# Two hybrid layers with paired heads, GpSimd scales and an earlier output projection, and a tail in halves

## The reference, cut to what matters

```python
p = rmsnorm(x, norm_g) @ w_in                       # 1024 -> 3488
(cq, ckv, kr, g_a, c_h, c_b, c_c, g_b, sg_u, sg_v, g_c, mq, mk, mv, g_d) = split(p)
q  = rmsnorm(rmsnorm(cq, .) @ mla_w_uq per head);   kv = rmsnorm(ckv, .) @ mla_w_ukv
o_a = causal_attention(rope(q), [rmsnorm(k_nope), rope(rmsnorm(kr))], v_a)   # 4 heads of 96
o_b = c_b * short_conv(c_c * c_h, conv_w)           # width 3, causal
o_c = sg_u * (tril(sg_w) @ layernorm(sg_v) + sg_b)  # chunks of 128 rows
o_d = causal_attention(rope(rmsnorm(mq)), rope(rmsnorm(mk)), mv)             # 4 heads of 64
x  = x + concat(o_a*silu(g_a), o_b*silu(g_b), o_c*silu(g_c), o_d*silu(g_d)) @ w_out
```

## Time and profile before

| | |
|---|---|
| median of 3 runs | 1792.18 us |
| profiled execution | 1790.85 us |
| its span, first to last instruction | 1788.9 us |
| TensorE busy | 1665.5 us, 93% |
| VectorE, ScalarE, GpSimd busy | 76%, 61%, 3% |
| mean granted TensorE clock | 0.966 |

### The profile page before, as it was taken

The page is one execution under the profiler, slowest core; times in us unless marked ns, Lnnn a source line. Parts: engine busy times, 40 slices in busy tenths (PEclk is TensorE's granted clock), DMA queues, the critical chain, the costliest instruction groups (busy, mean ns, idle before and its releaser), DMA issues.

```text
span 1788.9 us, 22550 instructions
## 1 busy us (share of the span) xinstructions
PE 1665.5 (93%) x7707; PEld 1374.0 (77%) x7707; DVE 1356.2 (76%) x1672; ACT 1086.1 (61%) x1308; POOL 47.8 (3%) x106
## 2 busy tenths in 40 slices
PE   6886987899899999799999999999999999999995
PEld 4665865688788888678888788888788887788884
DVE  4655675556654565789899799898898998898997
ACT  3343434356443446267777687777777777777773
POOL 2001000000100010100000000000000000000000
PEclk9897999799999999799999999999999999999998
DMA  9423542253454564359999899999899999899992
GB/s 331 140 94 94 172 137 75 77 188 104 156 177 155 187 217 135 125 201 370 381 352 371 302 357 372 355 370 347 312 371 376 358 360 350 310 371 368 363 359 105
DMA packets 153643, 462.71 MB, mean 259 GB/s; under 512 B 7807, under 2 KB 12173, under 8 KB 153405
## 3 DMA queue, kind: packets, MB, share of 16 engines
q1 hardware_dynamic: 151120, 454.32, 70.9%
q0 software_dynamic: 1696, 5.08, 1.1%
q10 hardware_dynamic: 716, 1.85, 0.3%
HBM read 460.18 MB, written 1.05 MB: 258 GB/s over the span
## 4 chain that ended last, share of the span: by engine, by line
PE 83%; DVE 7%; issue 4%; DVEq 3%; ACT 2%; POOL 0%; POOLq 0%; ACTq 0%
PE ps L2148 17%; PE ps L2150 17%; PE ps L2149 17%; PE ps L1686 8%; PE ps L1688 8%; PE ps L1687 8%; PE ps L2175 1%; PE ps L2082 1%; DVE wlo_sb L971 1%; PE ps L1711 1%; PE ps L2096 0%; PE ps L2097 0%; DVE wlo_sb L979 0%; ACT whi_sb L664 0%; PE ps L2067 0%
## 5 line engine op out<-in xcount | busy, mean ns | idle before, releaser
L979 DVE TENSOR_TENSOR wlo_sb<-raw_sb,whi_sb 128x1024 fp32r<-128x1024 f32 x672 | 788.3, 1220 | 111.2 <-ACT whi_sb L672 104.2
L672 ACT ACTIVATE whi_sb<-raw_sb 128x1024 fp32r<-128x1024 f32 x672 | 674.8, 1053 | 247.0 <-PE ps L2150 246.9
L2148 PE MATMUL ps<-whi_sb,xlo_sb 128*128 128x512 f32 x896 | 353.3, 394 | 9.8 <-issue 7.3
L2149 PE MATMUL ps<-wlo_sb,xhi_sb 128*128 128x512 f32 x896 | 350.3, 391 | 0.0
L2150 PE MATMUL ps<-whi_sb,xhi_sb 128*128 128x512 f32 x896 | 350.2, 391 | 0.0
L971 DVE TENSOR_TENSOR wlo_sb<-raw_sb,whi_sb 128x1024 fp32r<-128x1024 f32 (+2 forms) x198 | 225.5, 1180 | 160.7 <-ACT whi_sb L664 159.0
L664 ACT ACTIVATE whi_sb<-raw_sb 128x1024 fp32r<-128x1024 f32 (+2 forms) x198 | 192.2, 1021 | 238.9 <-PE ps L1688 212.8
L1686 PE MATMUL ps<-whi_sb,xlo_sb 128*128 128x512 f32 (+2 forms) x608 | 244.2, 402 | 21.3 <-DVE xlo_sb L1018 6.4
L1687 PE MATMUL ps<-wlo_sb,xhi_sb 128*128 128x512 f32 (+2 forms) x608 | 238.3, 392 | 0.0
L1688 PE MATMUL ps<-whi_sb,xhi_sb 128*128 128x512 f32 (+2 forms) x608 | 238.2, 392 | 0.0
L2148 PEld LDWEIGHTS ps<-whi_sb,xlo_sb 128*128 128x128 f32 x896 | 169.0, 189 | 46.7 <-issue 9.8
(11 more groups left out here) (353 smaller groups left out, 1414.8 us busy)
## 6 DMA issues: line engine op xcount, KB each, us to landing
raw_sb<-moe_wg SPq DMA_DIRECT2D x115, 1024.0 KB, 6.8
raw_sb<-moe_wu SPq DMA_DIRECT2D x112, 1024.0 KB, 7.0
raw_sb<-moe_wd SPq DMA_DIRECT2D x112, 1024.0 KB, 7.1
raw_sb<-w_in SPq DMA_DIRECT2D x40, 1024.0 KB, 5.1
raw_sb<-w_out SPq DMA_DIRECT2D x16, 1024.0 KB, 5.0
raw_sb<-ffn_wg SPq DMA_DIRECT2D x10, 1024.0 KB, 5.2
raw_sb<-ffn_wu SPq DMA_DIRECT2D x10, 1024.0 KB, 5.1
raw_sb<-ffn_wd SPq DMA_DIRECT2D x10, 1024.0 KB, 5.1
```

The costliest lines, as they stand in the source:

```text
L672: nc.scalar.activation(whi[i % SPLIT][:, c:c + KC // 2, :], raw[i % RAW][:, c:c + KC // 2, :], ACT.Copy).then_inc(hi_ready, 1)
L979: op = V.tensor_tensor(wlo[i % SPLIT][:, c:c + KC // 2, :], raw[i % RAW][:, c:c + KC // 2, :], whi[i % SPLIT][:, c:c + KC // 2, :], ALU.su ...
L2148: mm(out, lo, whi[q % SPLIT][:, w, :], start=first, stop=False)
L2149: mm(out, hi, wlo[q % SPLIT][:, w, :], start=False, stop=False)
```

## The change

- Column blocks come in another order; the last block is the narrow one. The inner y rows (o_b and o_c) are projected first, by two chunks of four row blocks; the outer ones (o_a, o_d) by two chunks of two row blocks and all 1024 columns. Both accumulators stay open over them.
- Heads go in pairs ("duos"): scores of two heads, one mask addition, one pair of maxima, two copies of transposes, and so on, each pair behind another chunk, in the functions that the mixers already used (now shared). The product with v comes in halves of four heads.
- The latents are transposed before their norm; ScalarE evacuates them with the gain, and the row scales come in with its squares and with v; q and k are normed per head anyway, by a factor that GpSimd multiplies in.
- GpSimd does all inverse roots of the layer (latents, heads, block heads, layer norm), the rope of kr, the products of the convolution (with its taps put on the input), and the products with the gates.
- Silu of each gate follows its block. In the FFN it goes ahead of the split of chunk 6.
- At the end yghi and yglo are made in halves, the scatter goes half by half, ScalarE squares one tile, and the output is scaled and stored by tiles.

The orders, and GpSimd's new function, which runs behind `row_scale_pool(pool, l + 1)`:

```diff
-HYBRID_ORDER = (0, 4, 5, 6, 3, 1, 2)
+HYBRID_ORDER = (0, 4, 5, 3, 2, 1, 6)
+Y_BLOCKS = (2, 3, 4, 5, 0, 1, 6, 7)
+HYBRID = column_chunks("in", D_IN, HYBRID_ORDER) + [Chunk("out", n * NC, NC, 2, KC, n, True, False) for n in range(2)] + [
+    Chunk("out", 0, 2 * NC, k, 2, 0, False, k > 0) for k in (0, 6)]

+        def hybrid_pool(pool, l):
...
+            pool.wait_ge(lat_seed, l + 1)
+            rsqrt_steps(pool, stat[:, 0:6], rs[:, 0:6], rs_tmp2[:, 0:6]).then_inc(lat_scale, 1)
...
+            G_.tensor_copy(kc[:, :, :, 64:96], kr.unsqueeze(2).to_broadcast([PART, TILES, 4, 32])).then_inc(kr_ready, 1)
+            pool.wait_ge(head_seed, l + 1)
+            rsqrt_steps(pool, stat[:, 24:40], rs[:, 24:40], rs_tmp2[:, 0:16])
...
+            op.then_inc(head_scale, 1)
+            pool.wait_ge(moba_seed, l + 1)
+            rsqrt_steps(pool, stat[:, 6:22], rs[:, 6:22], rs_tmp2[:, 0:16]).then_inc(moba_scale, 1)
+            pool.wait_ge(ln_seed, l + 1)
+            rsqrt_steps(pool, stat[:, 22:24], rs[:, 22:24], rs_tmp2[:, 0:2]).then_inc(ln_scale, 1)
+            pool.wait_ge(gate_c_ready, l + 1)
+            evacuated(pool, ("h", l, "b", 3))
+            G_.tensor_tensor(seg("sg_u"), seg("sg_u"), seg("g_c"), ALU.mult).then_inc(sug_ready, 1)
+            evacuated(pool, ("h", l, "b", 4))
+            evacuated(pool, ("h", l, "b", 5))
+            pool.wait_ge(mqk_ready, l + 1)
+            G_.tensor_tensor(z2, seg("c_h"), seg("c_c"), ALU.mult)
+            pool.drain()
+            G_.tensor_tensor(seg("c_c"), z2, tap[1], ALU.mult)
+            G_.tensor_tensor(seg("c_h"), z2, tap[0], ALU.mult).then_inc(conv_in_ready, 1)
+            pool.drain()
+            G_.tensor_tensor(z2, z2, tap[2], ALU.mult)
+            pool.wait_ge(gate_b_ready, l + 1)
+            G_.tensor_tensor(seg("c_b"), seg("c_b"), seg("g_b"), ALU.mult).then_inc(cb_ready, 1)
+            pool.wait_ge(gate_ad_ready, l + 1)
+            pool.wait_ge(o_ready, l + 1)
+            G_.tensor_tensor(y[:, :, 0:256], y[:, :, 0:256], seg("g_a"), ALU.mult).then_inc(ya_ready, 1)
+            pool.wait_ge(rden_ready, l + 1)
...
+                             .to_broadcast([PART, TILES, 4, HD]), ALU.mult).then_inc(gd_ready, 1)
```

ScalarE in a hybrid, from the evacuation of its third block on; `hi(i)` splits chunk i + 3:

```diff
+                proj(5)
+                act.drain()
+                nc.scalar.activation(mqk_sq, P[:, :, COLS["mq"][0]:COLS["mk"][1]], ACT.Square).then_inc(mqk_sq_ready, 1)
+                hi(5)
+                silu("g_c").then_inc(gate_c_ready, 1)
+                hi(6)
+                proj(7)
+                hi(7)
+                copy_T(1, QT[0:96, 0:4, :], tp[0:96, 0:2, :])
+                copy_T(2, KTr[0:96, 0:4, :], tp[0:96, 2:4, :])
+                hi(8)
+                proj(9)
+                act.drain()
+                silu("g_b").then_inc(gate_b_ready, 1)
+                act_exps(act, l, 0)
+                hi(9)
```

VectorE; `lo(i)` makes the low part of chunk i + 3:

```diff
+            latents(dve, l)
+            lo(3)
+            lo(4)
+            heads_stats(dve, l)
+            lo(5)
+            block_stats(dve, l)
+            heads_qk(dve, l)
+            lo(6)
+            dve.wait_ge(trig_ready, 1)
+            heads_rope(dve, l)
+            lo(7)
+            block_qk(dve, l)
+            gate_v_stats(dve, l)
+            lo(8)
+            dve_masked(dve, l, 0, mask)
+            dve_masked(dve, l, 1, mask)
```

TensorE from chunk 12 on (between `pe_duo_T` and `proj(13)` stand mix, behind `vn_ready`, and convolution, behind `conv_in_ready`):

```diff
+                proj(12)
+                pe.wait_ge(s_read, duo_at(l, 3))
+                pe_duo_T(pe, l, 0)
+                pe_duo_T(pe, l, 1)
...
+                proj(13)
+                pe.wait_ge(y_bc_made, l + 1)
+                pe.wait_ge(pT_ready, duo_at(l, 1))
+                pe_y_T(pe, l, range(0, 4))
+                pe_pv(pe, l, 0, tp[:, 3, :], v)
+                pe_open(pe, ("h", l, "n0"))
+                out(14, both, waits=True, done=True)
+                pe_duo_T(pe, l, 2)
+                pe.wait_ge(o_ready, l + 1)
+                pe_duo_T(pe, l, 3)
+                pe_open(pe, ("h", l, "n1"))
+                out(15, (0,))
+                pe.wait_ge(ya_ready, l + 1)
+                pe.wait_ge(pT_ready, duo_at(l, 2))
+                pe_y_T(pe, l, (4, 5))
+                pe_pv(pe, l, 1, tp[:, 3, :], v)
+                out(15, (1,), done=True)
+                pe.wait_ge(y_made, l + 1)
+                pe_y_T(pe, l, (6, 7))
+                out_wide(16, 0, both, waits=True)
+                out_wide(16, 1, both).then_inc(split_used, 1)
+                out_wide(17, 0, both, waits=True).then_inc(n0_summed, 1)
+                out_wide(17, 1, (0,))
+                pe_added(pe, ("h", l, "n0"))
+                pe_T(pe, T_X[l + 1] if l + 1 < DEPTH else T_MIX_X[0], 0, x)
+                out_wide(17, 1, (1,)).then_inc(split_used, 1)
```

The FFN on ScalarE, and the last job's yghi:

```diff
         def swiglu(before):
-                    act_hi(act, FFN, AT_FFN, i + SPLIT)
                     if i < n_up and i % 4 == (3 if i < 4 else 2):
...
                         last.then_inc(acc_free[0], 1)
+                    act_hi(act, FFN, AT_FFN, i + SPLIT)

+            for h in range(2):
+                nc.scalar.activation(yghi[:, h * NC:(h + 1) * NC], acc[:, 1, h, :], ACT.Copy).then_inc(yg_hi, 1)
```

More of the change, by code:

```diff
@@ L1713, in pe_T @@
             op.then_inc(xt_ps, 1)
-        def pe_in(pe, chunks, n_in, c0, name, nT, added, between):
-            for i in range(n_in):
-                chunk = chunks[i]
-                if chunk.first:
-                    pe_open(pe, name(chunk.block))
-                pe_chunk(pe, chunk, c0, i, acc[:, ACC_AT[name(chunk.block)][0]], x_lhs, TILES, nT=nT if i in (0, 2) else None)
-                if i == 0:
-                    if added:
-                        pe_added(pe, added)
-                    pe_T(pe, nT, 1, x)
-                between(i)
@@ new lines, in pe_proj, with pe_out @@
+        def pe_proj(pe, chunks, c0, i, name, nT):
+            name = name(chunks[i].block)
+            if chunks[i].first:
+                pe_open(pe, name)
+            pe_chunk(pe, chunks[i], c0, i, acc[:, ACC_AT[name][0]], x_lhs, TILES, nT=nT if i in (0, 2) else None)
+        def pe_out(pe, chunk, c0, i, g, att, at, tiles, ks, waits, done):
+            pe.wait_ge(lo_ready, c0 + i + 1)
+            for t in tiles:
+                for c in ks:
+                    k = at + c
+                    if waits and t == tiles[0]:
+                        pe.wait_ge(yt_lo, 8 * att + k + 1)
+                    hi, lo = x_lhs(k, t)
+                    first, last = chunk.first and c == 0, chunk.last and c == KC - 1
+                    mm(acc[:, g, t, :], lo, whi[i % SPLIT][:, c, :], start=first, stop=False)
+                    mm(acc[:, g, t, :], hi, wlo[i % SPLIT][:, c, :], start=False, stop=False)
+                    op = mm(acc[:, g, t, :], hi, whi[i % SPLIT][:, c, :], start=False, stop=last)
+            if done:
+                op.then_inc(split_used, 1)
@@ new lines, in pe_y_T, with head_qk @@
+        def pe_y_T(pe, att, blocks):
+            for c in blocks:
+                a = (c % 2) * S
+                for t in range(TILES):
+                    op = nc.tensor.transpose(tp[:, (c // 2) % 2, a + t * PART:a + (t + 1) * PART], y[:, t, y_cols(att, c)],
+                                             ident)
+            op.then_inc(yt_ps, 1)
+        def head_qk(att, h):
+            if att < DEPTH and h < 4:
+                return QT[0:96, h, :], KTr[0:96, h, :]
+            b, j = (h % 2) * HD, h // 2 + (2 if att < DEPTH else 0)
+            return QT[b:b + HD, j, :], KTr[b:b + HD, j, :]
@@ new lines, in out_wide @@
+                def out_wide(i, n, tiles, waits=False):
+                    g, last = ACC_AT["h", l, f"n{n}"][0], HYBRID[i].last
+                    pe.wait_ge(lo_ready, c0 + i + 1)
+                    for t in tiles:
+                        for c in range(2):
+                            k, w = (6 if last else 4) + c, 2 * c + n
+                            if waits and t == tiles[0]:
+                                pe.wait_ge(yt_lo, 8 * l + k + 1)
+                            hi, lo = x_lhs(k, t)
+                            mm(acc[:, g, t, :], lo, whi[i % SPLIT][:, w, :], start=False, stop=False)
+                            mm(acc[:, g, t, :], hi, wlo[i % SPLIT][:, w, :], start=False, stop=False)
+                            op = mm(acc[:, g, t, :], hi, whi[i % SPLIT][:, w, :], start=False, stop=last and c == 1)
+                    return op
@@ L1927, in mixer, with out, v @@
-                every = range(KC)
+                    pe_proj(pe, MIXER, at, i, name, T_MIX_X[m])
+                def out(i, part, tiles, ks, waits=False, done=False):
+                    pe_out(pe, MIXER[i], at, i, ACC_AT["m", m, part][0], att, MIXER[i].k0, tiles, ks, waits, done)
+                def v(h, t):
+                    return P[:, t, 1536 + h * HD:1536 + (h + 1) * HD]
+                every, both = range(KC), range(TILES)
                 proj(0)
@@ L2190, in tensor_program @@
                     job(b, j)
-            pe.wait_ge(acc_free[1], ACC_MOE[1] + 2 * n_pairs)
```

(11 more changed lines are left out.)

1065 lines of the change are left out of this document (517 added, 548 removed).

## The result

The changed kernel takes 1690.71 us (median of four runs, 1689.78 to 1692.13), the kernel before 1791.53 beside it: a ratio of 0.9439, with a 95% interval of 0.9427 to 0.9451. The profiled execution took 1690.24 us with a span of 1688.1; before they were 1790.85 and 1788.9.

What follows compares the result with a forecast made beforehand. TensorE was taken as the bound, losing time to waits and slow clock in the hybrids. 1790.85 less 75.9 (hybrids, after 10 for stalls), 6.4 (FFN) and 5.1 (end) gives 1703.4, stated as 1705 us; range 1696 to 1732.

Steps and rivals of the forecast that it cites:

- semaphores and lock-outs add; bounds 0 and 12, I take 5 each: minus 10: Both hybrids: chains leave 1 us of stall each; with semaphores and lock-outs 5 us each, 10 off the gain.
- slack for q and k: Hybrids: the q and k chain takes 20.7 us while TensorE has four chunks, 21.9 us; slack 1.2.
- Floor: A hybrid if nothing stops TensorE: matmuls and small products sum to 124.3 us, taken as 125.
- check by the clock: Hybrid 1: slow clock at 0.91 is 30 us; if all busy, 125.7 us remain; if all idle, floor 140.7.
- Hybrid 0: Falls from 176.0 to 132.4 us before stalls, keeping waits of 0.5 and 4.4 and about 2.6 of slow clock.
- FFN: Silu ahead of chunk 6's split removes 4.7 us idle and a slow stretch: gain 6.4 us.
- End: After the last matmul: earlier scatter, shared norm work and split store; last rows ready 1779.7 instead of 1784.45; gain 5.1 us.
- GpSimd's product: Hybrids: a GpSimd product of 512 columns takes 1.4 us, bounds 0.68 and 3.7.
- B: Rival: GpSimd is locked out by VectorE's subtractions, root chains take 13 instead of 4; 11 us more per hybrid, 1727; chance 0.18.
- C: Rival: ScalarE's one queue makes splits late behind Exp, copies and Silu; 10 us more per hybrid, 1725; chance 0.10.
- D: Rival: GpSimd's eight products per hybrid become the bound; TensorE waits from 2.7 us a product; at 11, 1808; chance 0.03.
- E: Rival: the change does not fill the gaps, waits only change names, FFN and end gains remain; 1781; chance 0.02.

Runs made afterwards that it cites:

- again: The changed kernel once more, unaltered: 1691.62 us, ratio 0.9450.
- ffn_back: Changed kernel with one edit undone: in the FFN ScalarE's Silu stands behind the split of chunk i + 3 again; 1697.72 us, ratio 0.9478.
- end_whole: Changed kernel with the end undone: yghi and yglo whole, one scatter, VectorE norms both tiles, one store; 1695.79 us, ratio 0.9471.
- pool_x2: Changed kernel with GpSimd's three products ahead of the convolution done twice each in every hybrid; 1699.64 us, ratio 0.9490.
- silu_late: Changed kernel with a hybrid's four Silu together behind the last column block, and GpSimd's sg_u and g_c product behind the convolution's three; 1713.93 us, ratio 0.9568.

## Why the prediction was wrong

*The step that failed* is "semaphores and lock-outs add; bounds 0 and 12, I take 5 each: minus 10". Nothing was added: TensorE has no wait of over 0.2 us between 48.64 and 361. In the profiled executions 1703.4 was forecast and 1690.24 came, 13.2 less: 10 for these stalls, 1.1 for the floor, 2.4 for the rest of hybrid 0, 0.2 for the FFN, 0.5 for the end, 0.6 for the start, less 1.5 in the experts' stretch and 0.2 around the span; the last us lies between profiled execution and median. The chains as worked out already held: 1.2 of slack for q and k against 1.45 measured (its parts add up to 11.1, not 11.2, so 1.3), 3.8 before the convolution against 2.9. A stall comes only where a chain passes its own slack, and lock-outs and semaphore delays of some tenths were smaller than every slack; the allowance had no row behind it, only caution. The range was to begin where no stalls are left, but without the 10 the sum is 1694.7, and 1696 was written; the measured 1690.7 lies 4.0 below even that sum, by the smaller terms that follow.

*Floor.* 125 against 124.45, 0.5 per hybrid; the bottom-up sum (124.3) was right to 0.2. The check by the clock was right to choose the busy time as slow.

*Hybrid 0.* 132.4 less stalls was to be 137.4; it took 129.2. Laid beside hybrid 1 matmul by matmul it is 4.8 longer: 1.9 at two short waits for low parts near its start (0.5 was kept), 2.9 at the first evacuation (a wait of 2.6; 4.4 was kept), and nothing for the clock (2.6 was kept). That the clock cost nothing is luck. The changed kernel's profile and that of again, the same kernel, at this place:

```profile
48.64 0.88 PE L1946 MATMUL ps<-con_sb,P_sb 128*128 128x128 f32 x6 [2.64 <-ACT P_sb L834]
...
49.82 0.40 PE L1801 MATMUL ps<-whi_sb,xhi_sb 128*128 128x512 f32 x1
```

```profile
47.83 1.54 PE L1946 MATMUL ps<-con_sb,P_sb 128*128 128x128 f32 x6 [2.60 <-ACT P_sb L834]
...
49.60 0.63 PE L1800 MATMUL ps<-wlo_sb,xhi_sb 128*128 128x512 f32 x1
```

The same wait, and in again 1.4 us of slow matmuls behind it. Of the twelve profiles with this wait of 2.6 us, seven show a stretch at half clock behind it, five do not.

*FFN* 6.4: 6.65 in the profile, 7.0 by ffn_back. *End* 5.1: 5.6 in the profile, 5.1 by end_whole. *Experts* 0: 1.5 lost. 0.8 of it is slow clock in the routing; the stretch takes 1023.2 to 1025.1 us in the runs with three-transfer borders and no late one, so the rest is no more than runs differ by. *Mixers* 0: right. GpSimd's product 1.4: 1.29.

*Rivals.* B's lock-outs are in the trace (13 of the 60 root steps of hybrid 1 take 0.5 to 1.1 us instead of 0.2) and, contrary to its price, free until a chain has no slack (pool_x2 shows the price then). C did not appear, and silu_late, which loads ScalarE's queue at its end, made no split late. D's mechanism was right and its point too high: 6.9 us for three products, 2.3 each, is where the wait begins, not 2.7. E fell: the gaps are filled.

Of what was to be seen in the profile, the signs came and the sizes were off: clock 1.00 in the hybrids, no wait at the copy of the probabilities, none at q and k, none before the second gate block; but 124.45 where 128 to 133 was named, and 129.2 for 135 to 140.

## What to carry to other kernels

Where one engine is to stay full, write for every hand-over when it is ready and when it is used, and let the smallest difference decide: as long as all are positive, an extra delay smaller than the slack costs nothing, and no allowance belongs in the sum; once one is negative, add to the wait between nothing and 2 us of slow clock behind a single wait of 2 to 4 us, and up to 5 behind a long one or two in a row. An engine off the path (GpSimd here) is worth using for its freedom, not its speed, but its long operations should not lie beside two-input operations of VectorE. And before a change of a few microseconds is judged, see whether an unrelated loop came to lie elsewhere: count the instruction transfers at its border.
